# Expert stage of a two-layer trunk: row selections and additions of an expert in blocks

## Chip, cores, metric

One core of a Trainium2 chip runs the whole program. The metric is device time in microseconds, the median of three runs. The engines are PE (TensorE, matrix products), PEld (its weight loads), DVE (VectorE), ACT (ScalarE), POOL (GpSimd) and SP (SyncE, which issues nearly all loads from memory here).

## What is computed

The program is a trunk of two layers on 256 tokens of width 1024, all in float32: a recurrent block with a dense channel mixer, then sliding-window attention with a mixture of eight experts. The change lies in the mixture alone. `lax.top_k` picks two experts for each token, and each expert is a SwiGLU of width 3584:

```python
def swiglu(h, w_gu, w_down):
    g, u = jnp.split(h @ w_gu, 2, axis=-1)
    return (jax.nn.silu(g) * u) @ w_down

def moe_swiglu(h, w_router, w_gu, w_down):
    ...
    top_v, top_i = lax.top_k(logits, TOP_K)
    top_w = jax.nn.softmax(top_v, axis=-1)
    gates = jnp.sum(jax.nn.one_hot(top_i, N_EXPERTS, dtype=F32) * top_w[..., None], axis=1)
    out = jnp.zeros_like(t)
    for e in range(N_EXPERTS):
        out = out + gates[:, e:e + 1].astype(t.dtype) * swiglu(t, w_gu[e], w_down[e])
    return out.reshape(bsz, seq, d)
```

The kernel computes for each expert only the tokens that chose it.

## The kernel before

**Places in the list.** Eight experts stand one behind the other, `e` = 0 to 7. Expert 0 is fixed; the others are sorted at run time by their number of tokens. A place has room for 96 tokens (three blocks of 32) or 64 (two blocks): e = 1, 4 and 7 have two blocks (`BLOCKS`, L67; `few` in the code), the others three.

**Halves and steps.** The width of 3584 is cut into two halves, t = 0 and 1. A half has a step "g" (gate), a step "u" (up) and a step "d" (down). `moe_order` (L416) puts the down step of a half behind the up step of the next half, so the order is g(e,0), u(e,0), d(e-1,1), g(e,1), u(e,1), d(e,0), g(e+1,0) and so on. All queues walk this one list, PE at L2099, ACT at L1050, DVE at L1574, SP at L663.

**Loads.** Each step uses eight loads of 896 KB. SP writes them into 18 slots; a slot is loaded again when PE has reported the load in it used (`unit_used`), and PE waits for a load by `unit_full`. A g or u step is eight steps over k, one load each (`in_step`, products of 32 columns of weights, four beside each other). A d step is 14 rows i, of 1024 values each, over its eight loads (`down_step`, L2080).

**Row selections.** POOL writes a 0/1 matrix `pick` for each expert. `pick_rows(e, k)` (L2052) multiplies chunk k of the token rows by it, two products on the full 128 by 128 array, which the trace shows as four instructions; eight such k make the input of expert e, in banks 3 and 4. ACT scales it into `xe` (`scale_rows`, L1003), eight operations. The products of the g step of expert e wait for that (`xe_scaled`).

**Turned slots.** To add an expert's result to the tokens' rows, `pick` has to be turned: `turn_pick(e)` (L2037) does it with two transposes on PE into bank 5, and ACT copies them to `selT` (`copy_turned`, L1011).

**Additions.** When the down products of expert e are through, DVE and ACT move them to `y` (`y_scale`, L1551; `y_out`, L1038). Four products `add_piece` (L2045; 512 columns each, two instructions in the trace) put them back at their tokens, into banks 3 to 6, and DVE adds each piece into `acc` (`add_rows`, L1560).

**Where these stand.** PE works strictly in the order of its code. In d(e,0) the two transposes for e come behind row 3 and the selections for expert e+1, one k each, behind rows 4 to 11. In g(e,1) the four additions of expert e-1 come behind k = 3, 4, 5 and 6. Banks 3 to 5 are also those of the up products, and bank 6 is half of the down products' pair, so these steps wait for DVE's product `hs` (`hs_ready`), and u(e,1) and d(e,0) wait for the additions (`added`).

Of the kernel before, what the change touches and what calls it, by code (L numbers as in the profile page):

```python
# [31 lines left out]
P = 128  # L32
D = 1024
SEQ = 256
KC = D // P
NB = SEQ // P
D_FF = 3 * D
FE = 7 * D // 2
E = 8
# [12 lines left out]
TB = 32  # L52
TBLKS = CAP // TB
SW = FE // 2
SUPERS = FE // SW
# [9 lines left out]
FEW = 3  # L65
CAP_FEW = 64
BLOCKS = [TBLKS] + [2 if r < FEW else TBLKS for r in SLOT_RANK]  # L67
ROW_TURN = 3
ROW_PICK = 4
ADD_STEP = 3  # L70
NEG = -1e30

TWO_PI = (6.28125, 0.0019350051879882812, 3.019916050561733e-07)
# [13 lines left out]
def build(nc, x, c, positions, inv_freq, ada_w, ada_b, mix_norm, ffn_norm, a_w_in, a_conv_w, a_conv_b,  # L87
# [3 lines left out]
    with ctx:  # L91
# [643 lines left out]
        def _(act):  # L735
# [275 lines left out]
            def copy_turned(e):  # L1011

                n = TB * BLOCKS[e]
                act.wait_ge(turn_mm, e + 1)
                nc.scalar.activation(selT[0:n, :], bank[5][0:n, 0:SEQ], ACT.Copy).then_inc(turn_set, 1)
# [34 lines left out]
            for s, (kind, e, t) in enumerate(moe_sets):  # L1050
                if kind != "g":
                    continue
                if t == SUPERS - 1 and e:
                    y_out(e - 1)
                (silu_of if three[e] else silu_few)(SUPERS * e + t, PER_SET * (s + 1))
                if t == SUPERS - 1:
                    copy_turned(e)
                    if e + 1 < E:
                        scale_rows(e + 1)
            y_out(E - 1)  # L1060

            def job(j, e, blk=0):
# [557 lines left out]
        def _(pe):  # L1620
# [421 lines left out]
                    last = transposed(bank[5][0:rows_of, n * P:(n + 1) * P], pick[:, n, e, 0:rows_of], ident[:, :])  # L2042
                last.then_inc(turn_mm, 1)

            def add_piece(e, p):  # L2045

                rows_of, (n, i) = TB * BLOCKS[e], pieces[p]
                pe.wait_ge(y_ready, 2 * e + i + 1)
                mm(bank[3 + p][:, :], selT[0:rows_of, n * P:(n + 1) * P], y[0:rows_of, 512 * i:512 * i + 512],  # L2049
                   start=True, stop=True).then_inc(add_mm, 1)  # L2050

            def pick_rows(e, k):  # L2052

                for n in range(NB):
                    ins = mm(picked(e, k), htok[:, n, k * P:(k + 1) * P], pick[:, n, e, 0:TB * BLOCKS[e]],  # L2055
                             start=n == 0, stop=n == NB - 1)
                return ins

            def in_step(banks, b, k, w, few=False):

# [38 lines left out]
            for s, (kind, e, t) in enumerate(moe_sets):  # L2099
                q, n0, few = SUPERS * e + t, PER_SET * s, not three[e]  # L2100
                if kind == "g":
                    after(pe, silu_ready, q)
                    if t == 0 and e == 0:
                        pe.wait_ge(counts_read, 1)
                        pe.wait_ge(xrow_done, 2 * NB)
                    elif t == 0:
                        pe.wait_ge(xe_scaled, e)
                elif kind == "u":
                    after(pe, hs_ready, q)
                    if e and t == 0:  # L2110
                        pe.wait_ge(turn_set, e)
                    elif e and t == SUPERS - 1:
                        pe.wait_ge(added, len(pieces) * e)
                else:
                    pe.wait_ge(hT_ready, q + 1)
                    if q == 0:
                        pe.wait_ge(g2_done, 2)
                    elif t == 0:
                        pe.wait_ge(y_ready, 2 * e)
                        pe.wait_ge(added, len(pieces) * e)  # L2120
                if kind == "d":
                    for i in range(ROWS):
                        for c in range(-(-4 * i // 7), (4 * i + 3) // 7 + 1):
                            arrive(n0 + c)
                        last = down_step(t, i, lambda c: moe_raw((n0 + c) % SLOTS), few)
                        if (4 * i + 4) // 7 > 4 * i // 7:
                            last.then_inc(unit_used, 1)
                        if t == 0 and i == ROW_TURN:
                            pe.wait_ge(hs_ready, q + 2)
                            turn_pick(e)  # L2130
                        if t == 0 and e + 1 < E and ROW_PICK <= i < ROW_PICK + KC:
                            last = pick_rows(e + 1, i - ROW_PICK)
                            if i == ROW_PICK + KC - 1:
                                last.then_inc(rows_mm, 1)
                    continue
                for k in range(KC):
                    arrive(n0 + k)
                    if s == 0 and k % 4 == 0:
                        pe.wait_ge(xe_ready, 1 + k // 4)
                    banks = gate_banks if kind == "g" else up_banks  # L2140
                    in_step(banks, e % 2, k, moe_raw((n0 + k) % SLOTS), few).then_inc(unit_used, 1)
                    if s == 2 and k == 4:
                        g2_rows()
                    if kind == "g" and t == SUPERS - 1 and e and 0 <= k - ADD_STEP < len(pieces):
                        add_piece(e - 1, k - ADD_STEP)

            def job(j, e, blk=0):

# [36 lines left out]
                        mm(bank[(2, 3, 6, 7)[2 * n + i]][:, :], selT[:, n * P:(n + 1) * P],  # L2185
                           y[0:CAP, 512 * i:512 * i + 512], start=True, stop=True).then_inc(back_mm, 1)

            pe.wait_ge(turn_set, E)
            for p in range(len(pieces)):
                add_piece(E - 1, p)  # L2190
            pe.wait_ge(added, len(pieces) * E)
            more_jobs(pe, job)

# [24 lines left out]
```

## Time and profile before

| | |
|---|---|
| median of three runs | 1347.38 us (1346.85 to 1352.85) |
| the profiled execution, its own time | 1348.28 us |
| its span on the core | 1346.5 us |
| PE busy | 1317.5 us, 98% of the span |
| DMA, mean | 355 GB/s; 417 to 419 GB/s in most slices of the expert stage |
| expert stage on PE | 492 us to 1340 us |

In the chain of waits each piece is a stretch of work on one engine and one line, with its start and length in us; pieces follow each other without a gap unless a piece of "issue" stands between them. L2069 are products of g and u steps, L2089 of d steps, L2055 the selections, L1624 transposes, L2049 the additions, L2025 the selections of expert 0 (in one block before its first step).

### The profile page before, as it was taken

The numbers are of one execution on the slowest core, as the hardware profiler recorded it, in microseconds if no ns is written. First come the engines' busy times: TensorE is split into PE (matmuls) and PEld (weight loads), VectorE is DVE, ScalarE is ACT, GpSimd is POOL, SyncE is SP. The second block draws the span as 40 slices with busy tenths as digits, with TensorE's granted clock in tenths as the row PEclk, the third lists the DMA queues.
The fourth block names the chain that finished last, engine by engine and source line by source line (L and its number), as shares of the span: only waits on it lengthen the run. The fifth ranks groups of instructions, "written<-read, shape, count | busy, mean of one in ns | idle before, by whom it ended". The sixth has DMA issues, their size and how long they took to land.

```text
span 1346.5 us, 27854 instructions
## 1 busy us (share of the span) xinstructions
PE 1317.5 (98%) x12266; PEld 787.5 (58%) x12267; DVE 577.4 (43%) x932; ACT 267.4 (20%) x496; POOL 13.0 (1%) x42
## 2 busy tenths in 40 slices
PE   7999899999998999999999999999999999999997
PEld 4888799999844863356344355544534444635543
DVE  2795898988767532223304122230320430403213
ACT  3572444444345430010010000001000001000000
POOL 1000000000000020000000000000000000000000
PEclk9999999999999999999999999999999999999999
DMA  9999668998954269989999999999999999999995
GB/s 352 354 384 336 226 206 310 318 317 319 386 195 188 85 257 404 383 330 419 419 418 418 419 418 418 413 386 366 419 419 418 418 418 419 418 406 336 418 418 236
DMA packets 129436, 477.62 MB, mean 355 GB/s; under 512 B 9408, under 2 KB 36256, under 8 KB 129312
## 3 DMA queue, kind: packets, MB, share of 16 engines
q1 hardware_dynamic: 129008, 475.23, 90.6%
q8 instruction: 98, 1.61, 0.5%
q10 hardware_dynamic: 304, 0.57, 0.1%
q14 instruction: 26, 0.21, 0.0%
HBM read 474.72 MB, written 1.05 MB: 353 GB/s over the span
## 4 chain that ended last, share of the span: by engine, by line
PE 93%; SPq 3%; ACT 1%; DVE 1%; issue 1%; DMA 0%; ACTq 0%; DVEq 0%
PE psum L2069 38%; PE psum L2089 20%; PE psum L1815 5%; PE psum L1816 5%; PE psum L1817 5%; PE psum L1731 3%; PE psum L2055 3%; PE psum L2049 2%; SPq L641 2%; PE psum L1880 2%; PE psum L1937 2%; PE psum L1769 2%; PE psum L1624 1%; PE psum L1861 1%; PE psum L1668 1%
## 5 line engine op out<-in xcount | busy, mean ns | idle before, releaser
L2069 PE MATMUL psum<-ring,xe 128*32 128x448 f32 x4704 | 454.5, 540 | 2.1 <-issue 1.9
L2069 PEld LDWEIGHTS psum<-ring,xe 128*32 128x32 f32 x4704 | 172.9, 110 | 273.4 <-issue 273.3
L2089 PE MATMUL psum<-ring,hT 128*32 128x256 f32 (+1 forms) x3180 | 255.1, 461 | 0.0
L2089 PEld LDWEIGHTS psum<-ring,hT 128*32 128x32 f32 x3180 | 143.0, 110 | 83.0 <-issue 28.1
L1477 DVE TENSOR_TENSOR hs<-sg,psum 128x1344 f32<-128x1344 f32 x10 | 15.5, 1554 | 324.8 <-PE psum L2069 324.8
L1815 PE MATMUL psum<-fh,dhi 128*128 128x256 f32 x384 | 110.6, 288 | 3.7 <-DVE fl L1284 2.5
L1492 DVE STREAM_TRANSPOSE hT<-hs 32x448 f32<-32x448 f32 x120 | 112.0, 944 | 1.6
L1816 PE MATMUL psum<-fl,dhi 128*128 128x256 f32 x384 | 109.2, 284 | 0.0
L1817 PE MATMUL psum<-fh,dlo 128*128 128x256 f32 x384 | 109.1, 284 | 0.0
L865 ACT ACTIVATE dhi<-ring 128x1024 fp32r<-128x1024 f32 x72 | 75.9, 1060 | 90.6 <-PE psum L1817 86.4
L1250 DVE TENSOR_TENSOR dlo<-ring,dhi 128x1024 fp32r<-128x1024 f32 x72 | 88.2, 1225 | 7.1 <-ACT dhi L865 4.9
L1815 PEld LDWEIGHTS psum<-fh,dhi 128*128 128x128 f32 x384 | 74.2, 193 | 5.0 <-issue 3.5
L1816 PEld LDWEIGHTS psum<-fl,dhi 128*128 128x128 f32 x384 | 74.3, 194 | 0.0
L1817 PEld LDWEIGHTS psum<-fh,dlo 128*128 128x128 f32 x384 | 74.2, 193 | 0.0
L1484 DVE TENSOR_TENSOR hs<-sg,psum 128x896 f32<-128x896 f32 x6 | 6.5, 1088 | 146.1 <-PE psum L2069 146.1
L1567 DVE SCALAR_TENSOR_TENSOR acc<-psum,tg,acc 128x512 f32<-128x512 f32 x32 | 24.0, 751 | 99.5 <-PE psum L2049 99.2
L2069 PE MATMUL psum<-ring_more,xe 128*32 128x448 f32 x672 | 66.6, 539 | 0.0
L1121 DVE SCALAR_TENSOR_TENSOR sqb<-ring,cact,sqb 128x512 f32<-128x512 f32 x84 | 63.0, 750 | 2.2
L1731 PE MATMUL psum<-H,ring 128*128 128x256 f32 x256 | 56.6, 380 | 0.4 <-ACT H L796 0.4
L1815 PE MATMUL psum<-gh,dhi 128*128 128x256 f32 x192 | 55.4, 289 | 0.0
L1031 ACT ACTIVATE sg<-psum 128x1344 f32<-128x1344 f32 x10 | 12.9, 1290 | 213.8 <-PE psum L2069 213.8
L1817 PE MATMUL psum<-gh,dlo 128*128 128x256 f32 x192 | 54.3, 283 | 0.0
(298 smaller groups left out, 1247.0 us busy)
## 6 DMA issues: line engine op xcount, KB each, us to landing
ring<-in_m_w_gu SPq DMA_DIRECT2D x224, 896.0 KB, 16.5
ring<-in_m_w_down SPq DMA_DIRECT2D x118, 896.0 KB, 16.2
ring<-in_ada_w SPq DMA_DIRECT2D x24, 2048.0 KB, 16.1
ring_more<-in_m_w_gu SPq DMA_DIRECT2D x32, 896.0 KB, 14.3
ring<-in_f_w_gu SPq DMA_DIRECT2D x24, 1024.0 KB, 14.2
ring<-in_f_w_down SPq DMA_DIRECT2D x6, 2048.0 KB, 14.7
ring_more<-in_m_w_down SPq DMA_DIRECT2D x10, 896.0 KB, 19.9
ring<-in_a_w_in SPq DMA_DIRECT2D x4, 2048.0 KB, 19.4
```

The costliest lines, as they stand in the source:

```text
L641: sp.dma_start(dst(ring[s]), src).then_inc(ring_full[s], 16)
L865: nc.scalar.activation(dhi[:, n % WB, :], dense_raw(t, part), ACT.Copy).then_inc(dhi_ready, 1)
L1121: then(v_.scalar_tensor_tensor(out=ada_acc(v), in0=w, scalar=cact[:, k:k + 1], in1=ada_acc(v), op0=ALU.mult, op1=ALU.add), asum if k == KC ...
L1250: v_.tensor_tensor(dlo[:, n % WB, :], dense_raw(*dense_steps[n]), dhi[:, n % WB, :].bitcast(F32), ALU.subtract).then_inc(dlo_ready, 1)
L1492: ins = v_.transpose(hT[32 * g:32 * g + 32, t % 2, :, TB * j:TB * j + TB], hs[TB * rows_:TB * rows_ + TB, seg, :].rearrange("p (s i) -> p ...
L1731: return mm(side_bank(T % 4)[:, SEQ * a:SEQ * a + SEQ], w[:, k, i * P:(i + 1) * P], H[:, k, :], **how)
L1815: mm(o, hi, xs[0], start=start, stop=False, skip_group_check=True)
L1816: mm(o, hi, xs[1], start=False, stop=False, skip_group_check=True)
L1817: return mm(o, lo, xs[0], start=False, stop=stop, skip_group_check=True)
L2055: ins = mm(picked(e, k), htok[:, n, k * P:(k + 1) * P], pick[:, n, e, 0:TB * BLOCKS[e]], start=n == 0, stop=n == NB - 1)
L2069: ins = mm(banks[TB * g:TB * g + TB, seg, 0:SEG], block(n), w[:, c0:c0 + SEG], start=first, stop=last, skip_group_check=True)
L2089: ins = mm(y_banks[TB * g:TB * g + TB, o0 + 256 * part:o0 + 256 * part + size], hT[:, t % 2, i, TB * b:TB * b + TB], raw(at // SW)[:, at % ...
```

## The change

The same products are issued, in another order, with other waits.

- The selections of an expert stand in one block of 16 products behind row 4 of a d step: for expert 1 in d(0,0), for expert e+2 in d(e,1). That is half an expert earlier than before.
- The two transposes for expert e stand right ahead of that block in d(e,1), where they stood in d(e,0).
- The four additions of expert e-1 stand in one block behind k = 4 of g(e,1). The block waits for the turned slots and for the scaled inputs of the next expert, which lie in the same banks.
- ACT copies the turned slots of e-1 and scales the inputs of e+1 ahead of moving the results of e-1, all before the silu of g(e,1).

```diff
 FEW = 3
 CAP_FEW = 64
 BLOCKS = [TBLKS] + [2 if r < FEW else TBLKS for r in SLOT_RANK]
-ROW_TURN = 3
 ROW_PICK = 4
-ADD_STEP = 3
+ADD_STEP = 4
 NEG = -1e30
 
 TWO_PI = (6.28125, 0.0019350051879882812, 3.019916050561733e-07)
...
                 if kind != "g":
                     continue
                 if t == SUPERS - 1 and e:
+                    copy_turned(e - 1)
+                    if e + 1 < E:
+                        scale_rows(e + 1)
                     y_out(e - 1)
                 (silu_of if three[e] else silu_few)(SUPERS * e + t, PER_SET * (s + 1))
-                if t == SUPERS - 1:
-                    copy_turned(e)
-                    if e + 1 < E:
-                        scale_rows(e + 1)
+                if t == SUPERS - 1 and e == 0:
+                    scale_rows(1)
+            copy_turned(E - 1)
             y_out(E - 1)
 
             def job(j, e, blk=0):
...
                     last = transposed(bank[5][0:rows_of, n * P:(n + 1) * P], pick[:, n, e, 0:rows_of], ident[:, :])
                 last.then_inc(turn_mm, 1)
 
-            def add_piece(e, p):
-
-                rows_of, (n, i) = TB * BLOCKS[e], pieces[p]
-                pe.wait_ge(y_ready, 2 * e + i + 1)
-                mm(bank[3 + p][:, :], selT[0:rows_of, n * P:(n + 1) * P], y[0:rows_of, 512 * i:512 * i + 512],
-                   start=True, stop=True).then_inc(add_mm, 1)
-
-            def pick_rows(e, k):
-
-                for n in range(NB):
-                    ins = mm(picked(e, k), htok[:, n, k * P:(k + 1) * P], pick[:, n, e, 0:TB * BLOCKS[e]],
-                             start=n == 0, stop=n == NB - 1)
-                return ins
+            def add_rows_of(e):
+
+                rows_of = TB * BLOCKS[e]
+                pe.wait_ge(turn_set, e + 1)
+                if e + 2 < E:
+                    pe.wait_ge(xe_scaled, e + 2)
+                for p, (n, i) in enumerate(pieces):
+                    if n == 0:
+                        pe.wait_ge(y_ready, 2 * e + i + 1)
+                    mm(bank[3 + p][:, :], selT[0:rows_of, n * P:(n + 1) * P], y[0:rows_of, 512 * i:512 * i + 512],
+                       start=True, stop=True).then_inc(add_mm, 1)
+
+            def pick_rows(e):
+
+                pe.wait_ge(pick_ready, NB * (e + 1))
+                for k in range(KC):
+                    for n in range(NB):
+                        last = mm(picked(e, k), htok[:, n, k * P:(k + 1) * P], pick[:, n, e, 0:TB * BLOCKS[e]],
+                                  start=n == 0, stop=n == NB - 1)
+                last.then_inc(rows_mm, 1)
 
             def in_step(banks, b, k, w, few=False):
 
...
                         pe.wait_ge(xe_scaled, e)
                 elif kind == "u":
                     after(pe, hs_ready, q)
-                    if e and t == 0:
-                        pe.wait_ge(turn_set, e)
-                    elif e and t == SUPERS - 1:
+                    if e and t == SUPERS - 1:
                         pe.wait_ge(added, len(pieces) * e)
                 else:
                     pe.wait_ge(hT_ready, q + 1)
...
                         last = down_step(t, i, lambda c: moe_raw((n0 + c) % SLOTS), few)
                         if (4 * i + 4) // 7 > 4 * i // 7:
                             last.then_inc(unit_used, 1)
-                        if t == 0 and i == ROW_TURN:
-                            pe.wait_ge(hs_ready, q + 2)
-                            turn_pick(e)
-                        if t == 0 and e + 1 < E and ROW_PICK <= i < ROW_PICK + KC:
-                            last = pick_rows(e + 1, i - ROW_PICK)
-                            if i == ROW_PICK + KC - 1:
-                                last.then_inc(rows_mm, 1)
+                        if i == ROW_PICK and (t or e == 0):
+                            if q + 1 < SUPERS * E:
+                                pe.wait_ge(hs_ready, q + 2)
+                            if t:
+                                turn_pick(e)
+                            if e + t + 1 < E:
+                                pick_rows(e + t + 1)
                     continue
                 for k in range(KC):
                     arrive(n0 + k)
...
                     in_step(banks, e % 2, k, moe_raw((n0 + k) % SLOTS), few).then_inc(unit_used, 1)
                     if s == 2 and k == 4:
                         g2_rows()
-                    if kind == "g" and t == SUPERS - 1 and e and 0 <= k - ADD_STEP < len(pieces):
-                        add_piece(e - 1, k - ADD_STEP)
+                    if kind == "g" and t == SUPERS - 1 and e and k == ADD_STEP:
+                        add_rows_of(e - 1)
 
             def job(j, e, blk=0):
 
...
                         mm(bank[(2, 3, 6, 7)[2 * n + i]][:, :], selT[:, n * P:(n + 1) * P],
                            y[0:CAP, 512 * i:512 * i + 512], start=True, stop=True).then_inc(back_mm, 1)
 
-            pe.wait_ge(turn_set, E)
-            for p in range(len(pieces)):
-                add_piece(E - 1, p)
+            add_rows_of(E - 1)
             pe.wait_ge(added, len(pieces) * E)
             more_jobs(pe, job)
```

PE in the first down step of expert 1 (d(1,0), two blocks), before: `pick,A` are selections, `ident,pick` transposes, `ring,hT` and `ring_more,hT` down products.

```order
L1624 MATMUL psum<-ident,pick 64x128 [waits pick_ready,hs_ready]
L1624 MATMUL psum<-ident,pick 64x128
L2089 MATMUL psum<-ring,hT 32x512 x4
L2055 MATMUL psum<-pick,A 128x96 x2
L2055 MATMUL psum<-pick,A 128x96 x2
L2089 MATMUL psum<-ring_more,hT 32x512 x4
L2055 MATMUL psum<-pick,A 128x96 x2
L2089 MATMUL psum<-ring_more,hT 32x512 [waits unit_full12]
L2089 MATMUL psum<-ring_more,hT 32x512 x3
L2055 MATMUL psum<-pick,A 128x96 x2
```

PE in d(1,1) now:

```order
L2097 MATMUL psum<-ring,hT 32x512 x7
L1625 MATMUL psum<-ident,pick 64x128 [waits pick_ready,hs_ready]
L1625 MATMUL psum<-ident,pick 64x128
L2063 MATMUL psum<-pick,A 128x96 [waits pick_ready]
L2063 MATMUL psum<-pick,A 128x96 x15
L2097 MATMUL psum<-ring,hT 32x256 [waits unit_full17]
L2097 MATMUL psum<-ring,hT 32x256 x3
L2097 MATMUL psum<-ring,hT 32x512 x6
L2097 MATMUL psum<-ring,hT 32x512 [waits unit_full0]
```

Eight pairs of selections between down rows have become one block of 16, for expert 3 instead of 2, in d(1,1) instead of d(1,0), behind the two transposes.

PE in g(2,1) before, where expert 1 is added (`y,rstd`; `ring,xe` are gate products):

```order
L2069 MATMUL psum<-ring,xe 32x448 [waits unit_full7]
L2069 MATMUL psum<-ring,xe 32x448 x11
L2049 MATMUL psum<-y,rstd 128x512 [waits y_ready]
L2069 MATMUL psum<-ring,xe 32x448 [waits unit_full8]
L2069 MATMUL psum<-ring,xe 32x448 x11
L2049 MATMUL psum<-y,rstd 128x512 [waits y_ready]
L2069 MATMUL psum<-ring,xe 32x448 [waits unit_full9]
L2069 MATMUL psum<-ring,xe 32x448 x11
L2049 MATMUL psum<-y,rstd 128x512 [waits y_ready]
L2069 MATMUL psum<-ring,xe 32x448 [waits unit_full10]
```

PE in g(2,1) now:

```order
L2077 MATMUL psum<-ring,xe 32x448 [waits unit_full8]
L2077 MATMUL psum<-ring,xe 32x448 x11
L2055 MATMUL psum<-y,rstd 128x512 [waits y_ready,xe_scaled,turn_set]
L2055 MATMUL psum<-y,rstd 128x512
L2055 MATMUL psum<-y,rstd 128x512 [waits y_ready]
L2055 MATMUL psum<-y,rstd 128x512
L2077 MATMUL psum<-ring,xe 32x448 [waits unit_full9]
L2077 MATMUL psum<-ring,xe 32x448 x11
L2077 MATMUL psum<-ring,xe 32x448 [waits unit_full10]
```

Four additions with a k of gate products between them have become four in a row, behind two waits more; three k follow them instead of one.

## Rows read from the trace of the kernel before

**Rows 1.** Page, part 1: PE's busy us, share of the span, instructions

```profile
PE 1317.5 (98%) x12266; PEld 787.5 (58%) x12267; DVE 577.4 (43%) x932; ACT 267.4 (20%) x496; POOL 13.0 (1%) x42
```

**Rows 2.** Waits from 500 us on, PE's: us in total, times, longest us

```profile
PE psum L2069 <- issue: 1.9, 2, 1.0
```

**Rows 3.** Chain of waits, undisturbed stretches: start us, us, what

```profile
591.07 24.12 PE psum L2069 x256
...
681.68 36.29 PE psum L2069 x384
...
717.97 12.07 PE psum L2089 x112
...
831.92 18.13 PE psum L2089 x192
```

**Rows 4.** Chain of waits, selections between three-block rows; wait behind two-block selections

```profile
680.73 0.95 issue
...
780.53 1.43 PE psum L2089 x12
781.96 0.61 PE psum L2055 x4
782.58 1.43 PE psum L2089 x12
```

**Rows 5.** Timeline, expert 0's selections in one block: start us, us, instructions

```profile
488.44 3.65 PEld L2025 LDWEIGHTS psum<-mask,A 128*128 128x128 f32 x32 [0.83 <-issue]
488.47 3.78 PE L2025 MATMUL psum<-mask,A 128*128 128x96 f32 x32 [0.37 <-DVE mask L1467]
```

**Rows 6.** Chain of waits, additions between k steps, two blocks, then three

```profile
639.34 1.06 PE psum L2049 x2
...
642.03 1.06 PE psum L2049 x2
...
739.06 1.05 PE psum L2049 x2
...
742.50 1.05 PE psum L2049 x2
```

**Rows 7.** Chain of waits, the last down products, and the last four additions

```profile
1314.59 20.84 PE psum L2089 x192
...
1336.28 3.68 PE psum L2049 x8
```

**Rows 8.** Page, part 5, DVE: count, busy us, mean ns of one, idle before

```profile
L1477 DVE TENSOR_TENSOR hs<-sg,psum 128x1344 f32<-128x1344 f32 x10 | 15.5, 1554 | 324.8 <-PE psum L2069 324.8
...
L1567 DVE SCALAR_TENSOR_TENSOR acc<-psum,tg,acc 128x512 f32<-128x512 f32 x32 | 24.0, 751 | 99.5 <-PE psum L2049 99.2
```

**Rows 9.** Timeline, ACT scaling the selected rows: start us, us

```profile
678.90 2.68 ACT L1007 ACTIVATE xe<-psum,mod,aff 128x96 f32<-128x96 f32 x8 [12.54 <-PE psum L2055]
```

**Rows 10.** DMA, 588:1332 us: GB/s in 40 slices of 18.6 us; loads' queue

```profile
GB/s 358 420 418 418 419 418 418 418 420 418 418 418 419 418 418 393 400 298 421 418 420 418 419 419 418 418 417 420 418 418 419 418 403 407 319 369 419 418 418 356
...
q1 hardware_dynamic: 47346, 301.66, 99.4%
```

**Rows 11.** DMA, the loads' queue in 598:904, 930:1200, 1288:1312: packets, MB, share

```profile
q1 hardware_dynamic: 19896, 126.78, 100.6%
...
q1 hardware_dynamic: 17635, 112.38, 100.9%
...
q1 hardware_dynamic: 1576, 10.04, 101.2%
```

**Rows 12.** SP's last six loads; then loads issued in 866:916 and 1060:1075 (median)

```profile
L668 SPq DMA_DIRECT2D ring<-in_m_w_down x6: 332/333/2250, 1300.5 to 1308.0; - x6
...
DMA to landing us min/median/max: 20.0/21.7/23.3
...
ring<-in_m_w_gu SPq DMA_DIRECT2D x14, 896.0 KB, 8.6
...
ring<-in_m_w_down SPq DMA_DIRECT2D x7, 896.0 KB, 24.1
```

## The prediction

> **What bounds the kernel now.** I read the page's busy times first: PE is busy for 98% of the span [rows 1]. Its waits from 500 us on come to 1.9 us before gate and up products [rows 2], and no load is among those that it waits for. So in the expert stage PE's own list of instructions sets the end, and everything taken out of that list counts, as long as the next resource can follow. The chain of waits gives prices without a cost model, since its pieces follow each other without gaps: undisturbed, a k of g or u takes 36.29/16 = 2.268 us with three blocks and 24.12/16 = 1.508 us with two; a row of d takes 18.13/14 = 1.295 us with three and 12.07/14 = 0.862 us with two [rows 3].
>
> The second thing to see is the DMA view, since it stands right behind PE. From 588 to 1332 us most slices read 417 to 421 GB/s, and only a few dip: 393, 400, 298 in the middle and 403, 407, 319, 369 towards the end [rows 10]. A queue that runs level in slice after slice is full; it is slack only in the dips. SP issues a load when PE frees its slot, so a faster PE first fills these dips, and then runs into the queue.
>
> **Part 1, selections in a block.** From one down row to the next, with a selection between them, it is 782.58 - 780.53 = 2.05 us, so a selection costs 2.05 - 1.295 = 0.755 us, though its four instructions show only 0.61 us; the row beside it has grown from 1.295 to 1.43 us [rows 4]. In one block the same kind of selection takes 3.78 us for 32 instructions, 0.118 us each [rows 5]. Four would be 0.47 us; the other 0.755 - 0.472 = 0.283 us is what going from column products to full products and back costs. Before: 7 experts x 8 x 0.755 = 42.3 us. After: 7 x (3.78 + 0.283) = 28.4 us. Gain 13.9 us. Bounds: the instructions keep their price between rows, 32 x 0.61/4 = 4.9 us and 0.14 for the row, 35.2 us, gain 7.1; or the block has no switch left, 7 x 3.78 = 26.5, gain 15.8. I take the middle, nearest to the block that the trace shows.
>
> **Part 2, transposes.** Eight pairs remain; six now share the switch of the block behind them: 6 x 0.283 = 1.7 us, between 0 and that. The other two (experts 6 and 7) cost what they did.
>
> **Part 3, half an expert earlier.** Behind the selections of a two-block expert PE stood still for 0.95 us [rows 4], because only two short rows followed the last selection, and ACT's eight scalings need 2.68 us [rows 9]. There are two such places (experts 1 and 4), and they are the 1.9 us of [rows 2]. The scaling now has the rest of a d step and the g and u steps behind it, so 1.9 us go. What is late next there is nothing on PE's side: the silu before it is long done.
>
> **Part 4, additions in a block.** Between two additions lie 742.50 - 739.06 = 3.44 us with three blocks, and 642.03 - 639.34 = 2.69 us with two [rows 6]; less a k each, an addition costs 1.17 or 1.18 us. 7 x 4 x 1.175 = 32.9 us. Four in a row take 3.68 us at the end of the kernel [rows 7]: 7 x 3.68 = 25.8 us. Gain 7.1 us. Bounds: four at the 1.05 us that they show between steps and one switch of 0.12, 30.2 us, gain 2.7; or 8 x 0.42, 23.5 us, gain 9.4 (0.42 is four in a row less one 0.3 us switch, over eight instructions). The last expert's additions stay as they are.
>
> **Waits that are added.** PE is in order, so behind each waits all of PE. The transposes wait for `hs` of the next expert's first half: DVE's product takes 1.55 us [rows 8] from the end of the u step, and five rows (4.3 us at the least) cover it. The block of additions waits for ACT: nine rows (7.8 us with two blocks) lie between the selections and the end of the d step, for the copy and 2.68 us of scaling; then five k (7.5 us) for the move to `y`. If that cover were gone, each us of ACT would cost a us, seven times. The u step waits for four additions on DVE, 4 x 0.75 us [rows 8], of which all but one run beside the block or in the three k behind it (4.5 us). I cost all of them at nothing. The wait for POOL's `pick` was passed a row earlier before, and SP issues nothing that it did not.
>
> **PE's sum**: 13.9 + 1.7 + 1.9 + 7.1 = 24.6 us, from 7.1 + 0 + 1.9 + 2.7 = 11.7 to 15.8 + 1.7 + 1.9 + 9.4 = 28.8 us. Alone it would end the last down products at 1335.4 (1314.59 + 20.84 [rows 7]) - 24.6 = 1310.8 us.
>
> **Where the queue cuts it off.** In 588 to 1332 us the queue moved 301.66 MB [rows 10]. In 930 to 1200 us, level throughout, it moved 112.38 MB in 270 us, 416.2 GB/s [rows 11]. At that rate 301.66 MB need 724.8 us, so of 744 us 19.2 are slack. The first slice (358 for 418, 2.7 us) and the last (356, 2.8 us) are the ends, where the queue fills and empties; 13.7 us lie in the dips. They can be filled: at the end of the first dip, near 915 us, four experts' selections and three blocks of additions are behind PE, 4 x 2.0 + 0.95 + 3 x 1.0 = 12 us, more than the 7 us that are empty there. The queue also starts 2.3 us earlier, since the d step before it loses 8 x 0.755 + 0.28 and gains 4.06. So its last load lands 16.0 us earlier. That load now lands at 1308.0 + 23.3 = 1331.3 us [rows 12]; then at 1315.3. What PE does with it is the last 1.75 of 14 rows, 1.5 us: 1316.8 us, against 1335.4 before, a gain of **18.6 us**. That is later than the 1310.8 of PE alone, so the queue decides, and PE waits some 6 us for loads in the last expert or two, where two blocks use loads fastest (1.5 us each). Bounds by the rate: 10.04 MB in 24 us is 418.3 GB/s, 3.6 us more; 126.78 MB in 306 us, with a little of the first dip in it, 414.3 GB/s, 3.3 us less [rows 11]. So 15.3 to 22.2 us, and below that only where PE's sum is smaller.
>
> The page "DMA: Bandwidth & Descriptors" of the Trainium skill, section "Bandwidth", has 425 GB/s measured for 16 MB. By that figure 301.66 MB would take an estimated 710 us and the queue would not cut anything off; no stretch of [rows 11] reaches it.
>
> **Rivals.**
> First, the queue keeps up and PE decides. It needs loads that land some 6 us sooner than at 416 GB/s, or dips that hold more than I counted; [rows 11] speak against the rate, and the 418.3 GB/s of the end come close. Gain 24.6 us, 1347.4 - 24.6 = 1322.8 us.
> Second, the change does less than it says: the 0.755 us is the price of a selection and not of the switch, and blocks cost what the pieces did. For it speaks that a piece's instructions alone show 0.61 of it; against it, the block of [rows 5], which is the same product. Gain 11.7 us by PE's lower bounds: 1335.7 us.
> Third, slower: blocks starve the queue. In a block PE frees no slot for about 4 us, where it freed one every 2 or 3 us. If less than 4 us of loads are in flight when a block starts, the queue stands idle, and the level queue cannot make it up: at most 7 x 4.06 + 7 x 3.68 = 54 us, less 18.6, 35 us slower, 1383 us. Loads land 8.6 us after their issue where the queue is thinnest, and 24.1 us where it is full [rows 12]; so more than a block is in flight, and more of it when PE is ahead.
>
> **How the numbers follow.** The profiled execution took 1348.28 us, 0.9 more than the median of 1347.38; the gain is taken off the median: 1347.4 - 18.6 = 1328.8 us. Chances: the queue decides 0.62; PE decides 0.17; blocks pay little 0.14, some of it so little that it is within 0.5%; the queue starves, or another wait eats it all, 0.07. Half a per cent, 6.7 us, is about what a measurement of this kernel can tell from no change. Faster by more than that 0.89, within it 0.06, slower 0.05. The range from 1322 to 1337 us takes in the queue's bounds (1325.2 to 1332.1) and the first two rivals' times, and leaves the third out.
>
> **What would show it.** Right: the block of selections takes about 4 us in the chain, the four additions about 3.7; the waits of 0.95 us are gone; the DMA slices near 900 and 1230 us read 417 to 419 GB/s; PE waits for loads, some 6 us in all, in the last expert. Wrong: waits of PE before the additions or behind row 4 (ACT or DVE not covered); dips of the DMA beside blocks (third rival); no waits for loads and an end near 1311 us less the tail (first); blocks of 5 us (second). A rate of the queue other than 416 GB/s moves the time by about 1.7 us for each GB/s.

## The result: 1.1% faster, and the queue of the loads decides

The changed kernel takes 1334.43 us (median of four, 1333.11 to 1336.84), the kernel before 1347.31 us; the ratio is 0.9894, 95% interval 0.987 to 0.9917. The profiled execution took 1333.11 us, its span 1330.8 us.

Part of the scatter lies ahead of what was changed, so the stage is best measured from its own start. The first gate products of expert 0 in the timeline (start us, us, instructions), before and after:

```profile
492.18 10.36 PE L2069 MATMUL psum<-ring,xe 128*32 128x448 f32 x108
```

```profile
490.56 11.86 PE L2077 MATMUL psum<-ring,xe 128*32 128x448 f32 x124
```

The last down products end where DVE begins to move `y`, in the chain of waits (start us, us), before and after:

```profile
1335.45 0.69 DVE y L1556
```

```profile
1319.92 0.69 DVE y L1557
```

From the one to the other the stage took 1335.45 - 492.18 = 843.27 us before and 1319.92 - 490.56 = 829.36 us after: **13.9 us less**. All stage times below are counted so. (The expectations of the last runs count from the end of the first k, some 2.5 us later.)

PE's own waits from 500 us on, after (us in total, times, longest us); they answer to [rows 2]:

```profile
PE psum L2097 <- DMA ring<-in_m_w_down: 6.8, 13, 1.1
PE psum L2077 <- DMA ring<-in_m_w_gu: 1.4, 3, 0.5
PE psum L2055 <- DVE y L1557: 0.9, 1, 0.9
PE psum L2097 <- DMA ring_more<-in_m_w_down: 0.5, 2, 0.3
```

The 1.9 us of "issue" are gone. In their place stand 8.7 us in 18 short waits for loads, all in the last expert; none of the waits that the change added shows (the 0.9 us before an addition is the last expert's, behind the stage, and is there in the kernel before too). The chain of waits, two stretches that answer to [rows 4] and [rows 6] (L2097 down products, L2063 selections, L1625 transposes, L2077 gate and up products, L2055 additions):

```profile
564.98 6.47 PE psum L2097 x60
571.45 3.71 PE psum L2063 x32
575.17 11.81 PE psum L2097 x132
...
709.20 4.31 PE psum L2097 x40
713.51 0.34 PE psum L1625 x2
713.85 3.55 PE psum L2063 x32
717.40 7.90 PE psum L2097 x72
725.30 11.28 PE psum L2077 x120
736.58 3.63 PE psum L2055 x8
740.21 24.94 PE psum L2077 x264
```

A block of selections is 3.71 us alone and 0.34 + 3.55 us with the transposes ahead of it; a block of additions is 3.63 us. The rows beside them grow by no more than 0.15 us: the second d step is 4.31 + 0.34 + 3.55 + 7.90 = 16.10 us, against 12.07 us of such a step without anything in it, so transposes and selections cost 4.03 us there.

The DMA view from 588 to 1319 us (GB/s in 40 slices of 18.3 us, then the loads' queue and that of PE's instructions: packets, MB, share of 16 engines), which answers to [rows 10]:

```profile
GB/s 409 418 418 419 419 418 419 417 419 418 419 419 418 418 419 418 419 417 418 419 419 418 419 418 419 418 418 418 419 418 418 419 418 418 419 418 417 419 420 226
...
q1 hardware_dynamic: 47253, 301.03, 99.7%
q8 instruction: 63, 1.03, 0.6%
```

The dips of before are filled: 38 slices in a row read 417 to 420. Only the last one is low, 226, and lower than the 356 of before.

### The profile page after: what moved, and what is told of

Its sections match the earlier page's. It is cut to its first block, busy times and chain, and to the rows that moved or that the text cites. A ratio compares the mean times of both kernels' runs of the same rounds, so it can differ in the third digit from the quotient of the medians.

```text
span 1330.8 us, 27861 instructions
## 1 busy us (share of the span) xinstructions
PE 1294.8 (97%) x12266; PEld 810.1 (61%) x12267; DVE 577.2 (43%) x932; ACT 267.4 (20%) x496; POOL 13.0 (1%) x42
## 4 chain that ended last, share of the span: by engine, by line
PE 90%; DMA 3%; SPq 3%; ACT 1%; DVE 1%; issue 1%; POOL 0%; ACTq 0%; POOLq 0%; DVEq 0%
PE psum L2077 36%; PE psum L2097 16%; PE psum L1816 5%; PE psum L1817 5%; PE psum L1818 5%; PE psum L1732 4%; SPq L667 3%; PE psum L1881 2%; PE psum L1938 2%; PE psum L1770 2%; PE psum L2055 2%; PE psum L2063 2%; DMA ring<-in_m_w_down 2%; DMA ring<-in_m_w_gu 2%; PE psum L1625 1%; PE psum L1632 1%
## 5 line engine op out<-in xcount | busy, mean ns | idle before, releaser
L2077 PE MATMUL psum<-ring,xe 128*32 128x448 f32 x4704 | 451.5, 539 | 1.4 <-DMA ring<-in_m_w_gu 1.4
L2077 PEld LDWEIGHTS psum<-ring,xe 128*32 128x32 f32 x4704 | 190.2, 110 | 252.0 <-issue 246.6
L2097 PE MATMUL psum<-ring,hT 128*32 128x256 f32 (+1 forms) x3180 | 247.6, 460 | 5.9 <-DMA ring<-in_m_w_down 5.7
L2097 PEld LDWEIGHTS psum<-ring,hT 128*32 128x32 f32 x3180 | 151.0, 110 | 95.8 <-issue 27.2
L864 ACT ACTIVATE dhi<-ring 128x1024 fp32r<-128x1024 f32 x72 | 75.9, 1060 | 90.9 <-PE psum L1818 86.1
L2077 PE MATMUL psum<-ring_more,xe 128*32 128x448 f32 x672 | 66.7, 539 | 0.0
L1817 PE MATMUL psum<-gl,dhi 128*128 128x256 f32 x192 | 54.3, 283 | 0.0
## 6 DMA issues: line engine op xcount, KB each, us to landing
ring<-in_ada_w SPq DMA_DIRECT2D x24, 2048.0 KB, 16.1
```

Of the source, the lines that this page charges most:

```text
L864: nc.scalar.activation(dhi[:, n % WB, :], dense_raw(t, part), ACT.Copy).then_inc(dhi_ready, 1)
L1817: mm(o, hi, xs[1], start=False, stop=False, skip_group_check=True)
L2077: ins = mm(banks[TB * g:TB * g + TB, seg, 0:SEG], block(n), w[:, c0:c0 + SEG], start=first, stop=last, skip_group_check=True)
L2097: ins = mm(y_banks[TB * g:TB * g + TB, o0 + 256 * part:o0 + 256 * part + size], hT[:, t % 2, i, TB * b:TB * b + TB], raw(at // SW)[:, at % ...
```

## Experiments

Theory A: the queue of the loads sets the end of the stage. Theory B, its rival: PE's list still sets it, and its saving was merely smaller than summed. Each half of the change alone, the loads made thinner, and PE's list made shorter tell them apart.

**Selections in blocks, additions spread.**

```diff
...
-                    if kind == "g" and t == SUPERS - 1 and e and k == ADD_STEP:
-                        add_rows_of(e - 1)
+                    if kind == "g" and t == SUPERS - 1 and e and 0 <= k - 3 < len(pieces):
+                        add_rows_of(e - 1, k - 3)
```

> The changed kernel with its four additions spread again behind k = 3 to 6 of the second gate step, as before the change; only the selections and transposes stay in their blocks. PE's list is about 7 us longer than in the changed kernel. Theory A (the loads' queue sets the end): PE's own saving is still 17 to 18 us, more than the 14 to 15.5 us that the queue lets through, so the time is within 2 us of the changed kernel's, some 13 us under before. Theory B (PE's list sets the end and its saving was only smaller than summed): the additions' share is missing, the gain is 6 to 9 us.

Measured: ratio 0.9889 (0.987 to 0.9909), stage 1324.43 - 495.21 = 829.2 us: all of the gain, without the additions' block. PE still waits for loads, only less (of its waits, the first row):

```profile
PE psum L2100 <- DMA ring<-in_m_w_down: 3.6, 8, 1.1
```

**Additions in a block, the rest as before.**

```diff
-ADD_STEP = 3
+ADD_STEP = 4
...
-                    if kind == "g" and t == SUPERS - 1 and e and 0 <= k - ADD_STEP < len(pieces):
-                        add_piece(e - 1, k - ADD_STEP)
+                    if kind == "g" and t == SUPERS - 1 and e and k == ADD_STEP:
+                        for p in range(len(pieces)):
+                            add_piece(e - 1, p)
```

> The kernel before with its four additions in one block behind k = 4; selections and transposes as before. Theory A: PE is the bound here (it would save about 7 us, less than the queue allows), so the gain is 6 to 7.5 us, and PE waits for hardly a load. Then selections alone and additions alone add up to 20 us or more, against some 13 to 15 of both together. Theory B: 3 to 5 us, and the two alone add up to the whole.

Measured: ratio 0.9942 (0.9925 to 0.9958), stage 1327.45 - 491.20 = 836.25 us, 7.0 us less than before. All waits of PE:

```profile
PE psum L2069 <- issue: 1.9, 2, 1.0
PE psum L2049 <- DVE y L1556: 0.9, 1, 0.9
```

No load is waited for, and the waits of "issue" are still there. So the halves are worth 14.0 and 7.0 us alone, 21 in sum, and 13.9 together. That is what a second resource looks like that stands a little behind the first: the gains do not add.

**Thinner loads, with the change and without.**

```diff
-                    sp.dma_start(moe_raw(n % SLOTS), moe_part(*weights_of(e), kind, t, c)).then_inc(unit_full[n % SLOTS], 16)
+                    w_ = SW // 2 if c == 7 and n >= SLOTS else SW
+                    sp.dma_start(moe_raw(n % SLOTS)[:, 0:w_], moe_part(*weights_of(e), kind, t, c)[:, 0:w_]).then_inc(unit_full[n % SLOTS], 16)
```

> The changed kernel, but of every eighth load (from the nineteenth on) only half of the columns is loaded, so 5 to 6% fewer bytes; PE works on what is left in the slots, so the result is not the reference's. Theory A: PE no longer waits for loads in the last expert, the time falls by a further 8 to 10 us, to about 1325 us (24 us under before). Theory B: the time stays within 2 us of the changed kernel's.

> The kernel before with the same thinner loads (half the columns of every eighth load left out). PE does not wait for loads in the kernel before, so both theories expect no change: within 2 us of before. Against the run above it gives what the change saves on PE alone: theory A 23 to 25 us, theory B 13 to 15.

Measured: with the change 0.9812 (0.9789 to 0.9834), stage 1307.50 - 490.80 = 816.7 us; without it 1.0008 (0.9995 to 1.0021), stage 1335.57 - 492.27 = 843.3 us. Fewer bytes give the kernel before nothing and the changed one 12.7 us. Its waits in the stage, all of them, and its page's GB/s (40 slices of 33.0 us):

```profile
PE psum L2056 <- DVE y L1558: 0.9, 1, 0.9
```

```profile
GB/s 349 356 386 335 241 200 308 323 314 324 377 248 121 137 213 366 354 331 418 417 418 418 417 417 407 344 332 397 417 418 417 417 418 415 357 340 373 419 418 169
```

The waits for loads are gone and the dips are back: with the queue out of the way, the change saves 843.3 - 816.7 = **26.6 us** on PE.

**A shorter list on PE.**

```diff
-                    mm(bank[3 + p][:, :], selT[0:rows_of, n * P:(n + 1) * P], y[0:rows_of, 512 * i:512 * i + 512],
+                    c_ = 512 if e == E - 1 else 32
+                    mm(bank[3 + p][:, 0:c_], selT[0:rows_of, n * P:(n + 1) * P], y[0:rows_of, 512 * i:512 * i + c_],
```

> The changed kernel, but the additions of the first seven experts take 32 of their 512 columns (the rest of the columns is left out, so the result is not the reference's). PE's list is some 20 us shorter still (7 x 3.6 us less what seven short blocks cost). Theory A (the loads' queue sets the end): next to nothing is gained, under 2 us against the changed kernel, since PE only waits longer for loads. Theory B (PE's list sets the end): 18 to 22 us less than the changed kernel, about 1314 us.

Measured: 0.9919 (0.9893 to 0.9945), stage 1325.09 - 496.36 = 828.7 us, 0.6 us less than the changed kernel, though the seven blocks take 1.01 us each in the chain instead of 3.63, 18.3 us less work on PE. Its time as a whole even rose; in the profiled execution the reason lies ahead of the stage (last section). PE's waits for loads:

```profile
PE psum L2098 <- DMA ring<-in_m_w_down: 11.8, 22, 1.1
PE psum L2078 <- DMA ring<-in_m_w_gu: 8.4, 17, 1.0
PE psum L2098 <- DMA ring_more<-in_m_w_down: 0.9, 4, 0.3
```

They grew from 8.7 to 21.1 us. Theory B has fallen: taking work off PE buys longer waits.

**Blocks, but not half an expert sooner.** Blocks at row 4 of d(e,0) and the thinner loads, so that PE decides.

```diff
...
-                        if t == 0 and i == ROW_TURN:
+                        if t == 0 and i == ROW_PICK:
                             pe.wait_ge(hs_ready, q + 2)
                             turn_pick(e)
-                        if t == 0 and e + 1 < E and ROW_PICK <= i < ROW_PICK + KC:
-                            last = pick_rows(e + 1, i - ROW_PICK)
-                            if i == ROW_PICK + KC - 1:
+                            if e + 1 < E:
+                                for k in range(KC):
+                                    last = pick_rows(e + 1, k)
                                 last.then_inc(rows_mm, 1)
...
```

> Blocks of selections and of additions as in the changed kernel, but the selections of expert e+1 and the transposes of e stay in d(e,0), behind row 4, so they are not half an expert sooner; with the thinner loads of the run before, so that PE alone sets the end (half of the columns of every eighth load are left out, the result is not the reference's). From its start the stage took 814 us with all of the change and thin loads. If the earlier place is worth something of its own: 1.9 us more for the two waits of 0.95 us, or more. If the blocks alone do it, since nine rows then follow the selections and cover ACT: within 1 us of 814.

Measured in one execution: stage 1307.15 - 490.89 = 816.3 us against 816.7. PE's waits:

```profile
PE psum L2050 <- DVE y L1557: 0.9, 1, 0.9
```

The earlier place is worth nothing of its own; the block at row 4 alone removes the 0.95 us waits, because nine rows then follow the last selection.

**The row sums of the gate later.** Four products of 1.9 us moved out of the part before 588 us, in which the queue is not full.

```diff
...
+                            if q == 1:
+                                pe.wait_ge(silu_ready, 3)
+                                g2_rows()
...
-                    if s == 2 and k == 4:
-                        g2_rows()
```

> The changed kernel with four products (the gate's row sums of 1.9 us, until now in the second gate step of expert 0) moved behind the selections in the second down step of expert 0, and DVE's use of them as well. Before about 588 us the queue is not full and PE sets the pace, behind that the queue does. Theory A: PE reaches the point from which the queue is full 1.9 us earlier, and the whole stage ends 1.5 to 2 us earlier. Theory B: PE's list is as long as before, so nothing changes.

> The changed kernel once more, on the same chip as the run below. 13 to 15 us under before; from its start the stage takes 826.5 to 827.5 us, of which the queue is full from 588 us on.

> The changed kernel with the gate's row sums in the second down step of expert 0, once more, on the same chip as the changed kernel. Its stage took 823.7 us in one look against 826.8. Theory A: 2 to 3 us less than the changed kernel in the medians as well, if what comes before the stage scatters evenly; theory B: no difference.

Measured: 0.9874 (0.9854 to 0.9894) the first time and 0.9888 (0.9868 to 0.9908) the second, beside the changed kernel at 0.9885 (0.9865 to 0.9904). The stages are 1322.70 - 496.45 = 826.25 and 1318.87 - 492.00 = 826.9 us, against 829.36 and 1321.24 - 492.04 = 829.2 us: 2.3 to 3.1 us less in the two pairs. That has the sign of theory A and is more than its 1.5 to 2 us; by the kept traces (next experiment) the queue's leading engine is through 2.2 and 1.8 us earlier, about as theory A has it, and the other 0.9 and 0.5 us are a smaller distance between the engines. The second expectation, 2 to 3 us in the medians, was not met. In the medians (1333.78 against 1334.22 us) that does not stand out from the scatter ahead of the stage, so it is not shown to be faster as a whole.

**Who slows the loads.** The next section tells, at the term of the queue, why this came up: the loads came later than the bytes per us said. The kept traces hold what no view prints: the time of each of the 16 steps by which a load raises its semaphore, read here as one for each of the 16 DMA engines. PE waits for the last step. In the changed kernel the last step of a load comes 1.6 us behind its first near 590 us, 7.5 us near 930 us and 13.8 us for the last load, eight of the 16 steps within the last 2.9 us. Theory C: the packets that fetch instructions share engines with the loads, and a load lands with its slowest engine. Theory D: they cost nothing.

More fetches: 12000 register moves on POOL.

> The changed kernel with 12000 register moves on POOL behind its selection matrices, where it has nothing else to do: they touch no data, but have to be fetched (64 bytes each estimated from PE's 24500 instructions in 1.61 MB, so 0.77 MB, some 47 packets of 16 KB). Theory C: instruction fetches use the same DMA engines as the loads, on about half of them, and each costs its engine 1.1 us, so that loads, which land with their slowest engine, come later than the bytes per us say: the last load lands 3 to 6.5 us later, and so does the end. Theory D: fetches cost the loads nothing worth measuring: within 1 us.

Measured: 0.9883 (0.9859 to 0.9907), stage 1319.51 - 490.71 = 828.8 us. But the page has the same fetches as that of the changed kernel:

```profile
q8 instruction: 98, 1.61, 0.5%
```

No packet was added, so this run says nothing on C or D.

The very last load in 16 pieces of 8 rows:

```diff
...
+                    if n == E * UNITS - 1:
+                        for r in range(0, P, 8):
+                            sp.dma_start(dst[r:r + 8, :], src[r:r + 8, :]).then_inc(last_full, 16)
+                        continue
...
```

> The changed kernel with its very last load (896 KB) issued as 16 pieces of 8 rows instead of one of 128. The DMA traffic at the end of the changed kernel falls to half its rate for some 13 us while loads still land in step, as if half of the engines had run ahead and were through. If a piece of 8 rows goes to the same 8 engines each time, those get 112 KB each and the others none: the end moves by up to 4 us, earlier if they are the ones that ran ahead (theory C), later if they are the ones behind. If pieces spread over all engines, or no engine is ahead (theory D): within 1 us, but for a few us of issuing on SP.

Measured: 0.9926 (0.9902 to 0.995), stage 1329.50 - 496.16 = 833.3 us, 4.0 us more. SP's issues (start us, us), and GB/s from 1300 to 1340 us in slices of 1 us:

```profile
1275.84 22.62 SPq L673 DMA_DIRECT2D ring<-in_m_w_down  x10
1298.64 9.40 SPq L671 DMA_DIRECT2D ring<-in_m_w_down  x16
```

```profile
GB/s 430 416 416 430 416 416 416 330 237 222 201 222 222 186 172 229 217 215 229 208 222 201 172 65 50 50 36 0 0 0 0 8 0 272 328 311 162 0 8 0
```

The pieces were all issued by 1308.0 us, but traffic went on at half rate and then at 36 to 65 GB/s until 1327. The pieces' own semaphore rises in 144 steps, nine a piece, so a piece does not spread over all 16 engines. 79 of the steps had come by 1314 us, and 32 came from 1322.9 us on: some of the engines used were ahead and some behind. And the pieces disturbed the loads ahead of them: from 1308 to 1314 us the loads' packets took 0.43 to 0.53 us on the mean instead of 0.28, and the last step of a whole load fell from 13.7 to 16.8 us behind its first. So the 4.0 us decide nothing between C and D. By the Trainium skill, page "DMA: Bandwidth & Descriptors", section "Why a DMA increments its semaphore by 16 and not by 1", a DMA of 8 rows from SP uses the eight lowest-numbered engines. The trace does not name engines, so no run here shows which they are.

Fewer instructions: half of the column groups of g and u left out.

```diff
-                    for g in range(4):
+                    for g in range(2):
```

> The changed kernel with two of the four column groups of every gate and up product left out (half of those products; the result is not the reference's), so that PE waits for loads all along and the queue alone sets the pace; PE also has some 5400 instructions fewer in the stage (about a quarter of those it has there), and fewer packets that fetch them. From its start the stage takes 827 us in the changed kernel. Theory A: about the same, 822 to 828 us, since no load was saved. Theory C (fetches cost the slowest DMA engine 1.1 us each, spread over about eight engines): some 20 fetches fewer, 2 to 3 us less than otherwise. Theory B (PE's list sets the end): 200 us less.

Measured in one execution: 1332.0 us, stage 1318.51 - 492.95 = 825.6 us, 3.8 us less. The expectation was wrong on PE: four column groups run beside each other, so two of them take as long. Two three-block steps in the chain (two pieces, 35.96 us; 36.08 us in the changed kernel), PE's waits for loads, and the fetches from 588 to 1319 us:

```profile
675.34 35.67 PE psum L2077 x190
711.10 0.29 PE psum L2077 x2
```

```profile
PE psum L2097 <- DMA ring<-in_m_w_down: 6.2, 12, 1.1
PE psum L2097 <- DMA ring_more<-in_m_w_down: 0.6, 2, 0.3
```

```profile
q8 instruction: 45, 0.74, 0.4%
```

PE's pace is the same within 1%, its waits are less, and the bytes of the loads are the same; 45 packets of fetches instead of 63 went through, and the loads came 3.8 us sooner. That fits C (18 packets) a little better than its own 2 to 3 us, and not D. Halving the products also halves what PE reads of the slots, and this is one execution, so by itself it does not settle C.

The steps of the loads settle it. Counted from the stage's start, the first step of the last load comes at 813.49 us in both kernels, and its last step at 827.3 us in the changed kernel and 823.5 us here: the leading engine gained nothing, the late ones gained 3.8 us. In the changed kernel the distance from first to last step grows in jumps, the eight largest 0.7 to 1.0 us each; before each of them another eight fetches had started since the one before, and each came 2 to 4 us behind a fetch. With fewer instructions the fetches came every 16.1 us instead of 11.4, the large jumps every 129 us instead of every 91, and again exactly eight fetches had started from one to the next; in the repeat of the changed kernel too it is eight each time. Summed over the 16 steps, the distance to the first grew by 1.70 us per fetch in the one (60 fetches behind 600 us) and by 1.76 in the other (43). So theory C holds: as the count of eight and the eight late steps say, the fetches go round eight engines, and each sets its engine's share of the loads back, for as long as the queue stays full. Why by 1.7 us and not by the 1.1 us of the packet stays open.

## Why the prediction was right, point by point

**What bounds what.** Right: it said that the queue would cut PE's gain off, that the dips would fill, and that PE would wait some 6 us for loads in the last expert. It waits 8.7 us there. The last loads and PE's products in step (timeline; the bracket is the wait before a row and what ended it):

```profile
1311.44 1.07 PE L2097 MATMUL psum<-ring,hT 128*32 128x512 f32 x8 [0.20 <-DMA ring<-in_m_w_down]
1313.60 1.94 PE L2097 MATMUL psum<-ring,hT 128*32 128x512 f32 x20 [1.10 <-DMA ring<-in_m_w_down]
1315.76 1.92 PE L2097 MATMUL psum<-ring,hT 128*32 128x512 f32 x16 [0.22 <-DMA ring<-in_m_w_down]
1317.92 1.94 PE L2097 MATMUL psum<-ring,hT 128*32 128x256 f32 x20 [0.24 <-DMA ring<-in_m_w_down]
```

**PE's sum.** Forecast 24.6 us (11.7 to 28.8), measured 26.6 us with the thinner loads. The block of selections was priced 3.78 + 0.283 us and is 3.86 us where it stands alone (6.47 + 3.71 + 11.81 = 21.99 against 18.13 us), with the transposes 4.03 us; the additions, priced 3.68 us, are 3.63 us, and 725.30 to 765.15 us less the 36.08 us of two plain steps is 3.77 us. The waits of 0.95 us went as forecast, but for another reason than the one it gave: the block and not the earlier place.

**The added waits.** Cost nothing, as forecast: none of them is among PE's waits.

**The term that was mis-sized** is the queue's: 18.6 us forecast, 13.9 measured. The last load was to land 16.0 us earlier. It landed at 1294.5 + 23.3 us (the last issue, and the time from issue to landing of that load), 1317.8 us, which is 827.3 us from the stage's start, against 839.1 before: 11.8 us. That is 4.2 of the 4.7 us that are missing; the other 0.5 us is PE's work behind that load, 2.0 us instead of 1.5. As a rate of bytes the 416.2 GB/s were right: slices 2 to 39 read 417 to 420 with the fetches in them. The mistake was to price landings by that rate and to take the last slice for an end that stays as it is. It held back 2.8 us before; now (418 - 226)/418 x 18.3 = 8.4 us, which is 5.6 us more, and 16.0 - 5.6 = 10.4 us is close to what is left. GB/s of the last stretch in slices of 0.5 us (1300 to 1320 us, after) and of 1 us (1300 to 1340 us, before):

```profile
GB/s 444 416 387 459 387 430 444 330 315 301 244 272 258 244 201 258 258 205 215 215 186 215 229 186 201 229 229 186 229 186 158 172 143 43 14 0 0 0 0 0
```

```profile
GB/s 437 403 409 423 416 416 423 409 430 423 409 423 423 418 409 423 416 416 416 423 423 416 423 423 416 432 401 409 301 179 43 0 0 0 0 0 0 8 0 291
```

Before, the rate stays at some 416 until 1328 us and falls within three slices. After, it halves at about 1304 us and stays near 220 for some ten us, while loads go on landing in step (the eleven last: 23.1 to 25.1 us from issue to landing). Half of the engines were through and the others were not: the first of the 16 steps of the last load comes at 1304.1 us and the last at 1317.9 us. A rate in GB/s counts the engines that run ahead; PE waits for those behind. Behind a stretch in which the queue ran empty they start level again: in the kernel before, the distance from first to last step is 6.0 us near 870 us, 0.5 us near 915 and 1240 us, in the two dips, and 2.6 us for the last load, against 13.8 us after a queue that is full for 700 us. Taken by their last steps, the loads of the changed kernel came every 2.22 us from 600 to 1300 us, 413 GB/s; at 1.7 us for each GB/s, the prediction's own price, that is some 5 us less than 416.2 gives, about what is missing. What sets the late engines back is the fetching of instructions (experiments); the prediction had no such term.

**The time.** Forecast 1328.8 us, range 1322 to 1337, measured 1334.43. Of the 5.6 us, 4.7 are the stage's (18.6 less 13.9); the remaining 0.9 us is less than what executions differ by ahead of the stage, up to 6 us.

**Rivals.** The first (the queue keeps up) is what the thinner loads made of it. The second (blocks pay little) has fallen with the blocks' prices. The third (blocks starve the queue) did not come: no slice between the first and the last dips under 417.

## What to carry to other kernels

Where one engine is busy without a gap, look at what stands right behind it before summing gains: here 26.6 us of saving met a queue that let 13.9 through, and half of the change gave all of it. Test it from both sides: thin the second resource (the gain grows) and shorten the first one's list (nothing happens). Price a queue by when its transfers land, counted over a stretch in which it is full, not by the bytes per us that went through; and ask what else goes through the engines that carry it.

## What the runs showed of the hardware

**Mixing shapes on PE costs 0.28 us each time** a full 128 by 128 product stands between products of 32 columns: 0.755 us against 3.71/8 = 0.46 us for the same four instructions, with the rows beside them 0.135 us shorter. It is a difference between two orders of the same products; why it arises no run shows. The Trainium skill, page "TensorEngine Tiling (Array Packing)", section "Key Properties", says that a change of tiling mode drains the engine; it gives no figure.

**Fetching instructions is not free for the loads.** From 588 to 1319 us 63 packets with 1.03 MB, 16 KB each, took 0.6% of 16 engines, 0.006 x 16 x 731/63 = 1.1 us each, and the loads fell 1.7 us behind for each, summed over the engines. The Trainium skill, page "Runtime: NRT & Kernel Launch", section "Instruction fetch mechanics", has the blocks of 16 KiB and a DMA queue of their own, and calls the cost mostly hidden; PE shows no wait for them here, but with 18 packets fewer the last load came 3.8 us sooner.

**The clock ahead of the stage.** The start of the stage lay between 490.6 and 496.5 us. In the changed kernel and in the run with short additions, from 428 us (stretch, length, then busy us and count of PE, PEld, DVE, ACT and POOL, granted clock, DMA share, GB/s):

```profile
428.00:435.00 7.00, 3.62 (x38) 2.51 (x30) 5.64 (x23) 5.99 (x22) 0.00 (x0) 1.00 0.97 382
435.00:442.00 7.00, 7.00 (x51) 5.66 (x50) 5.08 (x25) 3.39 (x13) 0.00 (x0) 1.00 0.64 269
```

```profile
428.00:435.00 7.00, 3.75 (x34) 1.59 (x26) 6.55 (x23) 6.00 (x15) 0.00 (x0) 0.91 0.76 272
435.00:442.00 7.00, 6.85 (x34) 5.65 (x35) 3.75 (x16) 3.62 (x15) 0.00 (x0) 0.60 0.91 383
```

In the one PE was granted its full clock from 435 to 442 us, in the other 0.60 of it on the mean, so part of the stretch ran at 1.2 instead of 2.4 GHz. It is the same code in both, and in both PE was busy for about half of the stretch ahead (3.62 and 3.75 of 7 us), so what made the clock fall in the one alone stays open. By these rows the lower clock cost an estimated 0.09 x 7 + 0.40 x 7 = 3.4 us of the 5.8 by which the stage starts later. That is why the stage was compared from its own start.
